# FFN up products of two column groups by seven quarter products in place of eight, with weight blocks summed in place in the raw buffers

## The reference

```python
D_MODEL, SEQ, DEPTH = 1024, 256, 2
D_FF = ((8 * D_MODEL // 3 + 255) // 256) * 256
...
    for l in range(DEPTH):
        ...
        mixed = (gate_a * y_a + gate_b * y_b) @ w_o[l]
        x = x + rmsnorm(mixed, post_mix_g[l])
        h = rmsnorm(x, pre_ffn_g[l])
        f = (jax.nn.silu(h @ w_ffn_gate[l]) * (h @ w_ffn_up[l])) @ w_ffn_down[l]
        x = x + rmsnorm(f, post_ffn_g[l])
    return x
```

## Time and profile before

| | |
|---|---|
| time, median of 3 runs | 818.06 us |
| profiled execution: its own time | 818.09 us |
| its span, first to last instruction | 816.3 us |
| mean granted clock of PE | 0.998 |
| PE busy | 805.7 us, 99% |
| DVE busy | 538.1 us, 66% |
| ACT busy | 428.3 us, 52% |
| POOL busy | 66.1 us, 8% |
| read from memory | 146.36 MB, 181 GB/s over the span |

### The profile page before, as it was taken

How to read it: one execution, slowest core, us unless ns; L and a number is a source line. 1 busy time by engine, 2 the same in 40 slices (tenths; PEclk the granted TensorE clock), 3 DMA queues, 4 the chain that set the end, 5 groups by cost and what they waited for, 6 DMA issues and landing times.

```text
span 816.3 us, 10484 instructions
## 1 busy us (share of the span) xinstructions
PE 805.7 (99%) x4298; PEld 677.1 (83%) x4298; DVE 538.1 (66%) x549; ACT 428.3 (52%) x559; POOL 66.1 (8%) x127
## 2 busy tenths in 40 slices
PE   8999999999999999999999999999999999999997
PEld 5897898888888888888879889988888888888885
DVE  5799898556666464645488869975568645645652
ACT  6467968634454343443445788875326434343431
POOL 2841000000220000000011100000003000000000
PEclk9999999999999999999999999999999999999999
DMA  9876454444449465653476735444554556555511
GB/s 290 255 245 205 147 176 158 155 155 155 141 168 309 155 221 196 203 169 141 155 224 213 260 128 182 155 159 155 186 172 155 189 198 227 186 191 182 194 52 51
DMA packets 80049, 148.09 MB, mean 181 GB/s; under 512 B 7185, under 2 KB 27777, under 8 KB 80002
## 3 DMA queue, kind: packets, MB, share of 16 engines
q1 hardware_dynamic: 80000, 147.42, 54.4%
q10 hardware_dynamic: 2, 0.00, 0.0%
HBM read 146.36 MB, written 1.05 MB: 181 GB/s over the span
## 4 chain that ended last, share of the span: by engine, by line
PE 91%; DVE 3%; POOL 3%; issue 1%; ACT 0%; DMA 0%; DVEq 0%; POOLq 0%; ACTq 0%
PE work L646 17%; PE work L647 17%; PE work L648 17%; PE acc L646 8%; PE acc L648 8%; PE acc L647 8%; PE work L638 3%; PE work L639 3%; PE work L640 3%; POOL turned_by L531 1%; PE work L786 1%; PE acc L711 1%; PE work L734 1%; PE acc L724 1%; DVE weights_lo L1324 1%
## 5 line engine op out<-in xcount | busy, mean ns | idle before, releaser
L1324 DVE TENSOR_TENSOR weights_lo<-weights_raw,weights_hi 128x2048 fp32r<-128x2048 f32 x132 | 302.1, 2293 | 155.5 <-ACT weights_hi L959 155.4
L959 ACT ACTIVATE weights_hi<-weights_raw 128x2048 fp32r<-128x2048 f32 x132 | 252.6, 1916 | 197.7 <-PE work L648 115.0
L646 PE MATMUL work<-weights_hi,act_a_hi 128*128 128x512 f32 x544 | 214.3, 394 | 0.0
L648 PE MATMUL work<-weights_hi,act_a_lo 128*128 128x512 f32 x544 | 212.0, 390 | 0.0
L647 PE MATMUL work<-weights_lo,act_a_hi 128*128 128x512 f32 x544 | 211.9, 390 | 0.0
L646 PEld LDWEIGHTS work<-weights_hi,act_a_hi 128*128 128x128 f32 x544 | 102.2, 188 | 21.9 <-issue 1.0
L648 PEld LDWEIGHTS work<-weights_hi,act_a_lo 128*128 128x128 f32 x544 | 102.1, 188 | 21.4
L647 PEld LDWEIGHTS work<-weights_lo,act_a_hi 128*128 128x128 f32 x544 | 102.2, 188 | 20.4
L646 PE MATMUL acc<-weights_hi,act_b_hi 128*128 128x512 f32 x240 | 94.2, 393 | 0.0
L648 PE MATMUL acc<-weights_hi,act_b_lo 128*128 128x512 f32 x240 | 93.5, 390 | 0.0
L647 PE MATMUL acc<-weights_lo,act_b_hi 128*128 128x512 f32 x240 | 93.4, 389 | 0.0
(11 more groups left out here) (178 smaller groups left out, 885.1 us busy)
## 6 DMA issues: line engine op xcount, KB each, us to landing
weights_raw<-in_w_in SPq DMA_DIRECT2D x43, 1024.0 KB, 5.2
weights_raw<-in_w_ffn_down SPq DMA_DIRECT2D x22, 1024.0 KB, 4.9
weights_raw<-in_w_ffn_gate SPq DMA_DIRECT2D x20, 1024.0 KB, 5.1
weights_raw<-in_w_ffn_up SPq DMA_DIRECT2D x20, 1024.0 KB, 5.2
weights_raw<-in_w_pa SPq DMA_DIRECT2D x8, 1024.0 KB, 5.0
weights_raw<-in_w_pb SPq DMA_DIRECT2D x8, 1024.0 KB, 5.0
weights_raw<-in_w_o SPq DMA_DIRECT2D x8, 1024.0 KB, 4.8
weights_raw<-in_w_ffn_gate SPq DMA_DIRECT2D x4, 512.0 KB, 4.0
```

The costliest lines, as they stand in the source:

```text
L646: mm(dst, xh, wh, start=first, stop=False)
L648: return mm(dst, xl, wh, start=False, stop=final)
L959: activate(w_hi[:, SLOT[n], :], raw[:, n % RAW, :], ACT.Copy).then_inc(hi_done.sem, 1)
L1324: v.tensor_tensor(w_lo[:, SLOT[n], :], raw[:, n % RAW, :], bits(w_hi[:, SLOT[n], :]), ALU.subtract).then_inc(split_done.sem, 1)
```

## The change

The up product of two column groups (1 and 2, then 3 and 4) is taken as a 2 x 2 product of blocks: two token tiles by two halves in depth, and two halves in depth by two column groups. By the scheme with seven products it needs seven quarter products of 12 matmuls each (`s_product`, plan entries ("s", 0) to ("s", 6) for the first unit and to ("s", 13) for the second) in place of eight. For this

- DVE forms x as a whole (hi plus lo) and four sums and differences of its blocks (`x_sums`), which ACT and DVE split like the rest (`x_sums_hi`, `x_sums_lo`), once per layer;
- the four weight blocks of a unit (`b` in the list of loads) stay in raw buffers, and DVE adds one to the other in place between the splits (`block_sum`), so that a unit makes seven splits out of four loads. Two tensors that lie idle in the FFN, `q_feat` (QT) and `lru_a` (AG), become raw buffers 3 and 4;
- ACT copies three partial results out of PSUM (`unit_copy`) and DVE adds them up (`unit_add`) ahead of the products with the silu. Others are added up in PSUM by further matmuls.

With it, the plan of the FFN is in another order, the use of the banks is written out with a bank number for each (`freed_by` gives the semaphore for the use before), the slots skip three places in place of one, and the gate's silu has four buffers. At the layer change, ACT makes the high part of the third panel ahead of a square, DVE makes the low parts of the third and fourth in two halves each, and PE starts on a half. The memory for x sums lies over `q_tok` and `lru_u`, so POOL clears the convolution's history again before layer 1.

PE, at the end of the first column group of layer 0: the last matmuls by ("fu", 1) on tile 1 and the first of ("fg", 2), before.

```diff
-    for c in range(groups):
-        plan += [("fg", 2 * c), ("fg", 2 * c + 1), ("fu", 2 * c), ("fu", 2 * c + 1)]
-        if c:
-            plan += [("down", 2 * c - 2), ("down", 2 * c - 1)]
-    plan.remove(("down", 2 * groups - 3))
-    plan += [("fgu", 0), ("fgu", 1)]
+    plan += [("fg", 0), ("fg", 1), ("fu", 0), ("fu", 1)]
+    plan += [("fg", 2), ("fg", 3), ("s", 0), ("s", 1), ("down", 0), ("s", 2), ("fg", 4), ("s", 3), ("fg", 5)]
+    plan += [("s", 4), ("s", 5), ("down", 1), ("s", 6)]
+    plan += [("fg", 6), ("fg", 7), ("s", 7), ("s", 8), ("down", 2), ("s", 9), ("down", 3), ("fg", 8), ("s", 10)]
+    plan += [("fg", 9), ("s", 11), ("down", 4), ("s", 12), ("down", 5), ("s", 13)]
+    plan += [("fgu", 0), ("fgu", 1), ("down", 6)]
     plan += [("down", j) for j in range(2 * groups - 3, 2 * groups + 1)]
     return plan
...
+    def two(name, n, b):
+        return [((name, n), b), ((name, n + 1), b + 1)]
+    uses += two("fg", 2, 2) + two("turn_f", 0, 0) + [(("sa", 0), 0), (("sb", 0), 1), (("sd", 0), 1)] + two("fg", 4, 2)
+    uses += two("fg", 6, 2) + two("turn_f", 2, 0) + [(("sa", 1), 0), (("sb", 1), 1)] + two("turn_f", 4, 2)
+    uses += [(("sd", 1), 1)] + two("fg", 8, 2)
+    uses += two("fgu", 0, 2) + two("turn_f", 6, 0) + two("turn_f", 8, 0) + [(("turn_f", 10), 2)]
...
-        skips = [AT["fg", 2 * c] for c in range(2, 2 + -NPAN % RING)]
+        skips = [AT["pa", 0], AT["pb", 0], AT["fgu", 0]][:-NPAN % RING]
...
+        PRODUCTS = [(0, 0), (0, 1)] + [p for c in (1, 3) for p in ((c, 0), (c + 1, 0), (c + 1, 1), (c, 1))]
+        PRODUCTS += [(GROUPS, 0), (GROUPS, 1)]
+        PRODUCT = {p: n + 1 for n, p in enumerate(PRODUCTS)}
...
+        def freed_by(use):
+            name, n = use
+            if name == "sa":
+                return f_up, PRODUCT[2 * n + 1, 1]
+            if name in ("sb", "sd"):
+                return s_added, 3 * n + (1 if name == "sb" else 2)
+            sig, first = FREED_BY[name]
+            return sig, first + n + 1
...
+        UP_AT = {1: (1, 0), 4: (2, 0), 5: (2, 1), 6: (1, 1)}
         SCORES_AT = [("gelu", 0), ("gelu", 2), ("gate_b", 0), ("gate_b", 2)]
         SOFTMAX_AT = [("gelu", 1), ("gelu", 3), ("gate_b", 1), ("gate_b", 3)]
+        TURNED_AT = {("fg", 2): 0, ("fg", 6): 1, ("s", 8): 2, ("fgu", 0): 3, ("fgu", 1): 4}
...
-                k = USE[name, n]
-                if k >= 4:
-                    before, m = USES[k - 4]
-                    freed, first = FREED_BY[before]
-                    pe.wait_ge(*freed.at(l, first + m + 1))
-                return work[k % 4]
+                if USED_BEFORE[name, n]:
+                    freed, m = freed_by(USED_BEFORE[name, n])
+                    pe.wait_ge(*freed.at(l, m))
+                return bank(name, n)
...
+                    for k in range(4):
+                        if i in (0, 1, 6):
+                            ks, cols = k + (0 if i == 0 else 4), slice(P if i == 6 else 0, 2 * P if i == 6 else P)
+                            xh, xl = xn_hi[:, ks, cols], xn_lo[:, ks, cols]
+                        else:
+                            which = {2: 0, 3: 2, 4: 3, 5: 1}[i]
+                            xh, xl = xs_hi[:, which, k, :], xs_lo[:, which, k, :]
+                        adds = i >= 3
+                        mm(dst[:, :], xh, wh[:, k, :], start=k == 0 and not adds, stop=False, skip_group_check=adds)
+                        mm(dst[:, :], xh, wl[:, k, :], start=False, stop=False, skip_group_check=adds)
+                        last = mm(dst[:, :], xl, wh[:, k, :], start=False, stop=k == 3, skip_group_check=adds)
+                    last.then_inc(panel_used.sem, 1)
...
+                for n in range(AT["fg", 2], AT["down", 2 * GROUPS - 3]):
+                    name, j = PLAN[n]
+                    if name in ("fg", "fgu"):
+                        if j % 2 == 0:
+                            gate_banks = [claim(l, name, j + t)[:, :] for t in range(NT)]
+                        elif name == "fg" and (j // 2) % 2 == 1:
+                            turn_f(j // 4)
+                        elif name == "fgu":
+                            turn_f(GROUPS - 2)
+                        t_product(name, j, gate_banks, xn_hi, xn_lo)
+                        if (name, j) == ("fgu", 1):
+                            turn_f(GROUPS - 1)
+                    elif name == "s":
+                        s_product(j // 7, j % 7)
+                        if j == 8:
+                            turn_f(2)
+                    else:
+                        if j == 0:
+                            pe.wait_ge(*x_done.at(l, 2))
                         for t in range(NT):
                             last = down_panel(j, t, j == 0, False)
                         last.then_inc(panel_used.sem, 1)
-                t_pair("fgu", 0, xn_hi, xn_lo, between=lambda: turn_f(GROUPS - 1))
...
+                def x_sums_hi():
+                    for i in range(4):
+                        act.wait_ge(*xs_summed.at(l, i + 1))
+                        done(activate(xs_hi[:, i, :, :], (s_first, s_third, s_second, s_fourth)[i], ACT.Copy),
+                             xs_hi_done, i + 1)
...
+                    next_hi(2)
                     act.wait_ge(*panel_used.at(l, NPAN))
                     norm(7, 7, acc[:, 2:4, :].rearrange("p b f -> p (b f)"))
-                    next_hi(2)
...
+                name, j = PLAN[n]
+                if name == "s" and j % 7 in (0, 2, 3, 4):
+                    block_sum(l, j // 7, j % 7)
+            def block_sum(l, u, i):
+                to, what = {0: (0, 2), 2: (0, 3), 3: (0, 1), 4: (2, 3)}[i]
+                dve.wait_ge(*raw_loaded[RAW_OF["b", 4 * u + what]].at(l, LOADED_AT["b", 4 * u + what]))
+                into = raw_slot(RAW_OF["b", 4 * u + to])
+                v.tensor_tensor(into, into, raw_slot(RAW_OF["b", 4 * u + what]), ALU.add).then_inc(summed.sem, 1)
...
+                def unit_add(u, odd, t):
+                    if odd:
+                        dve.wait_ge(*panel_used.at(l, AT["s", 7 * u + 1] + 1))
+                        dve.wait_ge(*s_copied.at(l, 3 * u + 1))
+                        done(v.tensor_tensor(p1_t, bank("sb", u)[:, :], p1_t, ALU.add), s_added, 3 * u + 1)
+                        dve.wait_ge(*s_added.at(l, 3 * u + 1))
+                        return p1_t
+                    name, part, i, m = ("sd", u2_t, 4, 2) if t == 0 else ("sa", p5_t, 5, 3)
+                    dve.wait_ge(*panel_used.at(l, AT["s", 7 * u + i] + 1))
+                    dve.wait_ge(*s_copied.at(l, 3 * u + 3))
+                    done(v.scalar_tensor_tensor(part, bank(name, u)[:, :], -1.0, part, ALU.mult, ALU.subtract),
+                         s_added, 3 * u + m)
+                    dve.wait_ge(*s_added.at(l, 3 * u + m))
+                    return part
+                def x_sums():
+                    def block(k, t):
+                        return x_whole[:, 4 * k:4 * k + 4, P * t:P * t + P]
+                    own(v.tensor_tensor(x_whole, bits(xn_hi[:, :, :]), bits(xn_lo[:, :, :]), ALU.add))
+                    done(v.tensor_tensor(s_first, block(1, 1), block(0, 1), ALU.subtract), xs_summed, 1)
+                    done(v.tensor_tensor(s_third, block(0, 0), block(0, 1), ALU.subtract), xs_summed, 2)
+                    dve.wait_ge(*xs_summed.at(l, 1))
+                    done(v.scalar_tensor_tensor(s_second, s_first, -1.0, block(0, 0), ALU.mult, ALU.subtract),
+                         xs_summed, 3)
+                    dve.wait_ge(*xs_summed.at(l, 3))
+                    done(v.scalar_tensor_tensor(s_fourth, block(1, 0), -1.0, s_second, ALU.mult, ALU.subtract),
+                         xs_summed, 4)
+                def x_sums_lo():
+                    for i in range(4):
+                        dve.wait_ge(*xs_hi_done.at(l, i + 1))
+                        done(v.tensor_tensor(xs_lo[:, i, :, :], (s_first, s_third, s_second, s_fourth)[i],
+                                             bits(xs_hi[:, i, :, :]), ALU.subtract), xs_split, i + 1)
...
+                    if name == "s" and j % 7 in UP_AT:
+                        c, t = UP_AT[j % 7]
+                        f_product(2 * (j // 7) + c, t)
+                    if (name, j) == ("fgu", 1):
+                        for t in range(NT):
+                            silu(GROUPS, t)
+                            f_product(GROUPS, t)
+                    if name != "wo" or j < 2:
                         panels_lo(n)
+                    if (name, j) == ("fg", 0):
+                        x_sums()
+                    if (name, j) == ("fu", 0):
+                        x_sums_lo()
+                    if (name, j) in TURNED_AT:
+                        f_lo_part(TURNED_AT[name, j])
...
-                    split_lo(l + 1, 2)
+                    split_lo_halves(l + 1, 2)
                     normed(l + 1, 1, rstd_done.at(l, 8), 1, 1)
-                    split_lo(l + 1, 3)
+                    split_lo_halves(l + 1, 3)
```

241 lines of the change are left out of this document (173 added, 68 removed).

## The result

The changed kernel takes 838.25 us (median of 4 runs, 836.95 to 839.26), the kernel before 817.97: a ratio of 1.0249, 95% interval 1.0231 to 1.0267. I had predicted 842 (830 to 854). In the profiled execution 836.95 stands against 818.09, spans of 835.2 and 816.3 us.

What follows compares the result with a forecast made beforehand. PE, busy 99% of the span, was taken to bound the kernel. 818.1 - 10.9 (48 matmuls) - 1.0 (layer change) + 2 x (12.1 stall + 2.0 clock + 4.0 units) = 842.4 us; predicted 842, range 830 to 854.

Steps and rivals of the forecast that it cites:

- The stall: Before ("fg", 2) in each layer, PE stands for f_product(0, 1), queued late on DVE: 12.1 us each, 24.2 in all.
- the in-place sum: First weight-block sum on DVE's queue ahead of the product: taken as 2.3 us, bounded by 1.2 and 4.6.
- Two signs that I had named: PE's wait of about 12 us per layer named DVE lru_uc; DVE over 80% busy in the unit stretch.
- The clock: Behind each stall the clock falls and PE restarts slowly: 2.0 us per stall, with 0 and 3.5 as ends.
- The units: Waits of PE in the seven-product units of the FFN: 4 us per layer, with 1 and 9 as ends.
- ("fg", 8) and ("down", 4): Panels in raw buffer 4's chain of loads and splits: late by 0.9 us and by 1.0 to 1.4 us.
- ("s", 6): In the unit, it waits for the third unit add, which DVE reaches behind two splits: late by about 1 us.
- The layer change: PE's waits for splits of q panels at the layer change shrink: 1.0 us gained, with 0 and 1.2 as ends.
- "Only the first stall counts": Rival: in the FFN the clock returns at once and the units keep up: 830 us, chance 0.13.
- "DVE- and load-bound units": Rival: in the units, raw buffer 4's chain and the block sums each push further: 854 us, chance 0.12.
- "Faster": Rival: DVE reaches f_product(0, 1) in time, so the stall before ("fg", 2) is 1 us: 812 us, chance 0.04.
- The inner 836 to 849: Whole kernel time in the likeliest case alone, with one of clock and units at an end, not both.

Runs made afterwards that it cites:

- experiment 1: Changed kernel with the product of column group 0, tile 1, moved on DVE's queue to right behind silu(0, 1): 822.0 us, ratio 1.0059.
- experiment 2: Changed kernel with banks 0 and 1 swapped with 2 and 3 from ("fg", 2) to the end of the FFN: 826.5 us, ratio 1.0104.
- experiment 9: Changed kernel with whole x and its four sums moved on DVE ahead of the split of ("fg", 2): 833.8 us, ratio 1.0195.
- experiment 4: Changed kernel with 50 extra matmuls per layer on PE before ("fg", 2), filling the stand: 835.1 us, ratio 1.0212.
- experiment 7: Changed kernel with the edits at the layer change undone: 840.0 us, ratio 1.0280.
- experiment 6: Changed kernel with edits of experiment 1 and experiment 2, first turn's parts earlier, x sums' low parts later, load of ("down", 4) asked for earlier: 818.1 us.
- experiment 8: Experiment 6 with x sums, f_product(0, 1), x sums' low parts, f_lo_part(0) and first unit add re-placed on DVE: 812.5 us, ratio 0.9934.
- experiment 11: Experiment 8 with the third unit add moved forward, and both parts of column group 2's turn ahead of the split of ("fg", 8): 811.5 us, 0.9928.

## Why the prediction was right

**The stall.** Right in place, cause and size: 11.5 us where I had 12.1. The terms on DVE's queue came out as priced, the in-place sum of 128x2048 too (2.28 us; I had taken 2.3, with 1.2 and 4.6 as ends). All steps ran start to start, which is 0.1 us under the durations that I had summed for most instructions; that is the 0.6. Experiments 1, 2 and 9 show the mechanism from three sides. The terms of the sum came out as predicted or smaller, so no large errors cancelled. Two signs that I had named did not come: the page names no releaser for the stands, and DVE's share in the units stays just under 80%.

**The clock.** I charged 2.0 per stall from the slow transposes at the start; 1.6 and 1.7 in the profile, 1.6 by experiment 4, and 1.9 and 2.9 behind the same stands in experiment 7. The charge lies inside this spread, and the rival in which it costs nothing is out. The column of the granted clock showed it this time, at 0.50 from 252 on, where at the program's start it had said 1.00 beside slow transposes. As the Trainium skill has it ("TensorE: Matmul & The Clock Gate", "HAM oscillation — how this bites in real kernels"), the burst behind such a gap starts cold; the trace agrees for the stands of 11.35 us (steps of 0.43 us from 258.91 on). Behind the shorter stands of experiments 1 and 6 the burst began at full clock, and the measurement decides there.

```profile
251.00:252.00 1.00, 0.00 (x0) 0.00 (x0) 1.00 (x1) 0.00 (x0) 0.00 (x0) 0.66 1.04 403
252.00:253.00 1.00, 0.00 (x0) 0.00 (x0) 1.00 (x2) 0.00 (x0) 0.00 (x0) 0.50 1.11 442
...
261.00:262.00 1.00, 1.00 (x5) 0.77 (x4) 0.00 (x0) 0.00 (x0) 0.00 (x0) 0.72 0.00 0
```

**The units** are the term that I sized too high: 4.0 per layer, and 2.7 measured, of which 0.9 is not waiting at all but longer steps, a term that the prediction did not have. Of the waits that I listed, ("fg", 8) and ("down", 4) came, a little smaller (predicted 0.9 and 1.0 to 1.4; a step longer by 0.6 and 0.9 in layer 0, 0.7 and 0.7 in layer 1). ("fg", 9) costs 0.2 in layer 0. ("s", 6), for which I had about 1, did not wait: the third unit add starts at 309.31 and PE's down panel lasts until 310.23, when ("s", 6) starts with no gap. DVE was not late there because it had worked through the long stand; in experiment 8, without the stand, the wait of 1.0 us that I had predicted is there. DVE's share was 79% from 264.9 to 377.0 (88.87 of 112.1 us), where I had 87% for a unit. Changed kernel, PE:

```profile
345.42 0.47 PE L753 MATMUL work<-weights_hi,act_a_hi 128*128 128x512 f32 x1 [0.43 <-DVE act_b_lo L1933]
...
363.23 0.50 PE L753 MATMUL acc<-weights_hi,act_b_hi 128*128 128x512 f32 x1 [0.76 <-DVE weights_lo L1510]
```

**The layer change.** -1.0 predicted, -1.02 measured, and +1.01 when undone. Against the earlier trace rows, the wait before the first q panel is gone (the 0.6 us for L1544 in the waits stand at the program's start); the matmul behind the turn at 429.31 starts at 430.44, a gap of 1.13 where it was 1.34, and the turn itself comes 0.29 us behind the matmul ahead of it.

**The rivals.** "Only the first stall counts" (830) fell by the clock and the units; "DVE- and load-bound units" (854) by waits of 1.8 us per layer. "Faster" named the right place, DVE's queue ahead of the product, but the product in time is not enough for its 812: with that alone (experiment 1) the kernel took 822.0. Only with the places behind it set right too does the change win, 0.9934 in experiment 8.

**The range.** The inner 836 to 849 doesn't follow from the ends that I gave. One term at an end makes 836.4 (units at 1) at the low side and 845.4 (clock at 3.5) or 852.4 (units at 9) at the high side. The forecast and the outer range do not hang on it.

## What to carry to other kernels

When a buffer's next user changes, write down who frees it and what stands ahead of that instruction on its in-order queue; moving one instruction of 0.7 us was worth 16 us here, and removing 48 matmuls 11. A long stall hides those behind it: after it is gone each next one in DVE's order came up (11.4, then 4.7, 2.8, 1.1, 0.9 us), so count on only part of a removed stall until the whole stretch has been ordered by when the full engine asks. And a wait that hangs on a chain of loads through one buffer did not go when what stands beside it was reordered (experiment 11: it moved one link on); asking for the load earlier took one away (experiment 6).
